# Reordered loads and casts, masks on VectorE and a one-hot last expert block in a hybrid conv, attention and MoE layer

## The chip, the cores and the metric

The kernel runs on the 8 cores of one Trainium2 chip. Each core computes one of the 8 batch elements by itself; nothing is exchanged. The metric is the device time in microseconds of the slowest core. Engines are named as in the profile: PE is TensorE (matmuls; PEld its weight loads), DVE is VectorE, ACT is ScalarE, POOL is GpSimd, SP is SyncE. Data come from HBM through 16 transfer engines per core. A transfer is issued from SP's queue or from POOL's; only POOL's can change the type, and the kernel uses it to load fp32 weights as bf16.

## What is computed

One layer of a diffusion backbone over 2048 latent tokens and 256 context tokens of width 1024:

```python
mod = silu(c) @ w_ada + b_ada            # shift, scale, gate for two sub-layers
h = rmsnorm(x) * (1 + sc1) + sh1         # and the same for the context tokens
b, cg, xin, q, k, v, ga, gb = split(h @ w_in)
ya = (b * conv3(cg * xin)) @ w_a         # gated short conv
yb = attention(q, k, v, window=128, context keys, sink) @ w_b
x = x + g1 * (sigmoid(ga) * ya + sigmoid(gb) * yb) @ w_o
h = rmsnorm(x) * (1 + sc2) + sh2
# MoE: the best of 4 groups, then the best 2 of its 8 experts
y = sum over the 2 experts of gate * (silu(h @ w_a[e]) * (h @ w_u[e])) @ w_down[e]
out = rmsnorm(x + g2 * y)
```

There are 32 experts; each has 1024 x 512 weights up and 256 x 1024 down, 3 MB in fp32. Both experts of a token lie in one group of eight.

## The kernel before

All work is recorded as operations of a small planner (class Sched, lines 38 to 380). Each has an engine, what it reads and writes, and an assumed cost; `order` runs a list scheduler over them, which at each moment starts, on every free engine, the oldest ready operation within a window of 300, and models two transfer rings. Its result is the fixed order of each engine's program, with semaphores between them. Engines run their programs strictly in order, so a transfer on POOL waits for everything ahead of it there. `weave` (line 381) mixes a main list of steps with a side list in proportion to given costs; `mix` (line 631) puts k cast steps among a list.

The stages, in order, for tokens in 4 chunks of 512 (16 tiles of 128):

- **Modulation** (lines 670 to 686): four 1 MB weights wad on POOL, x tiles 0 to 5 on SP.
- **First mixer stage** (lines 688 to 793): for each of 18 tiles `n1_step` normalises (square on ACT, scale on DVE, add on DVE or, for every third, POOL at line 699), transposes on PE and copies by ACT and DVE in turn into HT; `cx_step`, `proj_step` and `v_step` compute conv inputs, keys and values. `x_load` (line 606) fetches tile t+6 on SP when tile t is done, into 6 buffers.
- **Attention with conv** (lines 802 to 949): the six gate weights (wab, wsl 4 to 7; lines 802 to 804) are loaded; then q projections, `b_step` (three conv operations on DVE, one matmul, one multiply) and `mod2_step` (second modulation, with its own load) are woven with `att_steps`. `sc_step` multiplies the outer key blocks by a 0/1 mask on POOL (line 898).
- **Gates** (lines 964 to 1204): `gate_step` per chunk, woven with attention of chunks 2 and 3, the folding of g1 into w_o, `wo_step`, the second norm `n2_apply` (which writes the normalised rows to hd in HBM, line 1011) and routing.
- **Casts**: for 18 of the 32 experts the fp32 weights are copied to a bf16 tensor wbf in HBM beforehand, in 72 quarter steps (`pre_step`, line 622); quarter h waits for quarter h-3, the first three for the last x tile. PREK tells how many stand in each of five stages. The 18 are experts 6 to 15 and then every second one.
- **Routing end** (lines 1205 to 1266): ranks and one-hot tables give, per expert block of 256 token slots, the tokens to gather, the rows to scatter to and the gates.
- **Experts** (lines 1345 to 1435): 34 blocks in order (32 experts, 2 overflow blocks); the ring holds the weights of 6. Per block: `G` gathers 2 x 128 rows from hd (POOL), `T` transposes them on PE, `U` is up plus silu, `F` folds g2 into the down weights (DVE, line 1381), `Dn` is down with the gate on eviction, `O` scatters 2 x 128 rows into yd in HBM. `run_items` records them so that U(i), T(i+1) come before Dn(i-1), O(i-1), and the weights `W(i+5)` are loaded when block i-1 is done. Three further groups of overflow blocks lie behind branches (`emit_region`) and run only if an expert has more than 256 tokens.
- **Tail** (lines 1454 to 1494): yd holds for each token two neighbouring rows. `yload` (SP) brings a tile of both rows, 8 buffers, after all scatters. `sum_step` adds the two rows on PE through an identity, adds x on DVE and squares on ACT; `out_step` scales on DVE and stores.

## Time and profile before

| | us |
|---|---|
| median of 3 runs | 907.84 |
| lowest, highest | 907.0, 973.5 |
| the profiled execution, device time | 906.63 |
| its span in the trace (slowest core, core 2) | 904.7 |
| spans of the other cores | 882.5 to 897.1 |

The page of the profile gives busy time per engine, the span in slices with the granted clock of TensorE and the share of the transfer engines, the queues, the chain of work that ended last, the costliest groups of instructions, and the issued transfers with their time to landing. The trace behind it answers questions about a stretch, a line or an engine. A wait "A <- B" is time in which engine A stood idle until B released it. A transfer share of 1.0 means that all 16 engines were busy; matmul times are those of the pipeline and depend on the granted clock.

### The profile page before, as it was taken

How to read it: one execution, taken by the hardware profiler on the slowest of the kernel's cores; microseconds unless marked ns; L12 is line 12 of the kernel's file. 1: busy time of each engine (PE TensorE's matmuls, PEld its weight loads, DVE VectorE, ACT ScalarE, POOL GpSimd, SP SyncE). 2: the span in 40 equal slices, each digit the busy share in tenths (PEclk: the TensorE clock that was granted, in tenths of full speed). 3: DMA queues.
4: the chain of work that ended last, by engine and by line, in shares of the span. 5: the costliest groups of instructions: out<-in, count | busy, mean ns of one | idle time of the engine just before them, and what ended most of it. 6: DMA issues, size and time to landing. Idle time of an engine off the chain costs nothing. (4 is left out here: it accounts for less than half of the span.)

```text
span 904.7 us, 14299 instructions; the slowest of 8 cores (882.5 to 904.7 us)
## 1 busy us (share of the span) xinstructions
PE 751.6 (83%) x5494; PEld 422.5 (47%) x5494; DVE 532.2 (59%) x1054; ACT 379.1 (42%) x687; POOL 327.2 (36%) x383
## 2 busy tenths in 40 slices
PE   6887799898999999999999943899699959788461
PEld 2344455343455444454444422576476637556210
DVE  1548946799743656568698787644344334333197
ACT  2326422644466775424253341045245415344353
POOL 2021411335344754211211104267577637632200
PEclk9988999999999999999999965799899979989685
DMA  8994799999977899999988899379989999996498
GB/s 151 209 204 152 153 147 155 150 149 126 149 108 105 187 158 174 196 151 173 188 138 136 128 180 165 97 223 304 223 264 213 229 220 248 245 234 216 153 323 321
DMA packets 37007, 168.41 MB, mean 186 GB/s; under 512 B 11692, under 2 KB 13868, under 8 KB 28611
## 3 DMA queue, kind: packets, MB, share of 16 engines
q0 software_dynamic: 27136, 140.36, 80.6%
q1 hardware_dynamic: 9796, 27.06, 8.8%
q8 instruction: 46, 0.75, 0.4%
q14 instruction: 29, 0.24, 0.1%
HBM read 234.26 MB, written 58.72 MB: 324 GB/s over the span
## 5 line engine op out<-in xcount | busy, mean ns | idle before, releaser
L550 PE MATMUL ps<-sb 128*128 128x512 bf16 (+10 forms) x4452 | 685.8, 310 | 116.5 <-DVE sb L583 24.8
L550 PEld LDWEIGHTS ps<-sb 128*128 128x128 bf16 (+4 forms) x4452 | 361.9, 102 | 416.0 <-issue 79.1
L563 ACT ACTIVATE sb<-ps 128x512 bf16<-128x512 f32 (+4 forms) x385 | 211.2, 588 | 339.5 <-PE ps L550 247.6
L568 DVE TENSOR_TENSOR sb<-ps,sb 128x256 bf16<-128x256 f32 (+4 forms) x196 | 85.4, 446 | 159.3 <-PE ps L550 79.9
L563 ACT ACTIVATE sb<-ps,sb 128x512 bf16<-128x512 f32 x136 | 83.4, 687 | 53.1 <-PE ps L550 29.9
L1350 POOL DMA_INDIRECT sb<-hd,sb x68 | 74.7, 1098 | 77.3 <-PE ps L1362 49.6
L580 DVE SCALAR_TENSOR_TENSOR sb<-sb 128x1024 f32<-128x1024 f32 (+4 forms) x96 | 101.5, 1072 | 1.5
L1401 POOL DMA_INDIRECT yd<-sb x68 | 72.9, 1072 | 55.0 <-ACT sb L563 34.3
L565 ACT ACTIVATE sb<-sb 128x1024 bf16<-128x1024 f32 x50 | 52.8, 1055 | 89.6 <-DVE sb L568 56.1
L898 POOL TENSOR_TENSOR sb<-sb 128x512 bf16<-128x512 bf16 x60 | 66.7, 1121 | 61.4 <-ACT sb L563 61.0
L1381 DVE TENSOR_TENSOR sb<-sb 128x2048 bf16<-128x2048 bf16 x34 | 41.7, 1226 | 76.0 <-DMA sb<-wex 43.2
L568 DVE TENSOR_TENSOR sb<-sb 128x512 bf16<-128x512 f32 (+5 forms) x102 | 80.8, 798 | 1.4
L580 DVE SCALAR_TENSOR_TENSOR sb<-sb,ps 128x512 f32<-128x512 f32 (+2 forms) x74 | 47.8, 645 | 44.8 <-PE ps L550 35.4
L629 POOL DMA_DIRECT2D wbf<-wex x72 | 37.1, 517 | 99.4 <-DMA wbf<-wex 98.8
L568 DVE TENSOR_TENSOR sb<-sb,ps 128x512 f32<-128x512 f32 (+1 forms) x65 | 42.6, 677 | 30.4 <-PE ps L550 30.2
L583 DVE COPY sb<-ps 128x1024 bf16<-128x1024 bf16 (+3 forms) x84 | 53.1, 660 | 6.1 <-PE ps L550 4.3
L568 POOL TENSOR_TENSOR sb<-sb 128x1024 bf16<-128x1024 f32 x6 | 16.0, 2672 | 76.1 <-PE ps L709 41.2
L1362 PE MATMUL ps<-sb 128*128 128x128 bf16 x544 | 36.7, 220 | 2.5 <-DVE sb L583 2.5
L1362 PEld LDWEIGHTS ps<-sb 128*128 128x128 bf16 x544 | 33.6, 98 | 3.8 <-DVE sb L583 2.7
L577 DVE TENSOR_SCALAR sb<-sb 128x1 f32<-128x1 f32 (+4 forms) x54 | 16.2, 310 | 32.1 <-ACT sb L565 32.0
L571 DVE TENSOR_TENSOR sb<-sb 128x16 f32<-128x16 f32 (+9 forms) x62 | 31.2, 512 | 2.2 <-DMA sb<-wo 1.3
L563 ACT ACTIVATE sb<-sb 128x1 f32<-128x1 f32 (+5 forms) x52 | 13.3, 266 | 36.7 <-DVE sb L577 16.4
(52 smaller groups left out, 246.5 us busy)
## 6 DMA issues: line engine op xcount, KB each, us to landing
wbf<-wex POOLq DMA_DIRECT2D x72, 384.0 KB, 12.4
sb<-wbf POOLq DMA_DIRECT2D x18, 1536.0 KB
sb<-wex POOLq DMA_DIRECT2D x16, 1536.0 KB
sb<-wad POOLq DMA_DIRECT2D x12, 1024.0 KB, 21.2
sb<-x SPq DMA_DIRECT2D x16, 512.0 KB, 23.1
sb<-wsl POOLq DMA_DIRECT2D x8, 1024.0 KB, 32.6
sb<-x POOLq DMA_DIRECT2D x16, 512.0 KB, 12.4
sb<-yd SPq DMA_DIRECT2D x16, 512.0 KB, 12.8
```

The lines of the kernel that those rows point to most:

```text
L550: ins = e.matmul(o, lhsT=l, rhs=r, start=s0, stop=s1)
L563: S.op("act", lambda e: e.activation(out=out, in_=in_, func=func, scale=scale), reads=[in_] + list(extra), writes=w)
L565: S.op("act", lambda e: e.activation(out=out, in_=in_, func=func, accum_out=accum), reads=[in_], writes=w)
L568: S.op(eng, lambda e: e.tensor_tensor(out=out, in0=a, in1=b, op=op), reads=[a, b], writes=[out])
L580: S.op(eng, lambda e: e.scalar_tensor_tensor(out=out, in0=a, scalar=s, in1=b, op0=o0, op1=o1), reads=[a, b] + list(rd), writes=[out])
L583: S.op(eng, lambda e: e.tensor_copy(out=out, in_=a), reads=[a], writes=[out], fast=a.dtype == BF16)
L629: S.op("pool", lambda e: e.dma_start(out=o_, in_=i_), reads=[("wbf", h - PRED)] if h >= PRED else [("xl", 17)], writes=[("wbf", h)], dma=( ...
L898: S.op("pool", lambda e, p4=p4, m_=m_: e.tensor_tensor(out=p4, in0=p4, in1=m_.unsqueeze(1).to_broadcast([128, 4, 128]), op=ALU.mult), read ...
L1350: S.op("pool", lambda e, x_=x_, ix=ix: e.indirect_dma_start(out=x_, out_offset=None, in_=hd_d, in_offset=bass.IndirectOffsetOnAxis(ap=ix, ...
L1362: ins = e.transpose(psb[:, k * 128:(k + 1) * 128], x_[:, k * 128:(k + 1) * 128], identb)
L1381: S.op("dve", lambda e: e.tensor_tensor(out=wdv[r], in0=wdv[r], in1=G2b.unsqueeze(1).to_broadcast([128, 2, 1024]), op=ALU.mult), reads=[wd ...
L1401: S.op("pool", lambda e, q=q, ix=ix: e.indirect_dma_start(out=yd_d, out_offset=bass.IndirectOffsetOnAxis(ap=ix, axis=0), in_=YB[q], in_off ...
```

## The change

- **x loads**: tiles 6 to 17 are loaded by POOL instead of SP. All adds of the first norm are on DVE; three of four copies of a transposed tile are on ACT, one on DVE.
- **Casts**: the first three wait for x tile 8 instead of 17; ten stand among the steps of the first mixer stage, then 10, 16, 16, 14 and 6 in the five later ones.
- **Gate weights**: one load stands behind every fourth step of the attention stage's main list, between the second modulation's.
- **Conv**: its first operation is on ACT. **Masks**: on DVE.
- **Experts**: the order is all experts but 7, 15, 23, 31 (with the overflow blocks at 12 and 22), then these four. Cast are, of those after the first six, two of three, and the last four: still 18.
- **yd**: the first half of its rows holds a token's first expert, the second half its second; where the first is one of the four last ones the two are swapped (sign of the token number, array tks). Tokens of a tile are spread two by two, and hd is written accordingly.
- **Last block** (expert 31): not scattered. `Z` writes zero rows for its tokens, `last_tok` and `last_place` build a one-hot matrix PL from its token list, and `sum_step` adds it by two matmuls per half tile from SBUF.
- **End of the experts**: Dn and O of blocks 31 and 32 come before the next U; Dn of block 33 stands behind the branches. The yd loads (16 of 512 KB, each the rows of 256 tokens in one half) are recorded before the branches: three wait only for the first 30 blocks, the others for all but block 33. If an overflow group runs, it loads them again.
- **Sum**: for five tiles x is added on PE in fp32, squared by ACT and scaled by DVE from PSUM.
- **Planner**: a DVE operation with two large SBUF inputs is taken to wait for a running POOL operation; transfers still open at the branches stay in the model.

```diff
+XC = 8
...
-PREK = (14, 16, 16, 16, 10)
+PREK = (10, 16, 16, 14, 6)
...
+        two = eng == "dve" and sum(1 for k, c in rd if k is None and len(c) >= 64) >= 2
...
+                if o["two"]:
+                    ce += max(0.0, st["pb"] - t)
                 o["t"] = t
                 free[e] = t + ce
+                if e == "pool" and o["dma"] is None:
+                    st["pb"] = t + ce
...
-            sdma(xs[t % 6], src, ("xs", t % 6), also=[("xl", t)])
+            if t < 6:
+                sdma(xs[t % 6], src, ("xs", t % 6), also=[("xl", t)])
+            else:
+                gdma(xs[t % 6], src, ("xsg", t % 6), also=[("xl", t)])
...
-        pre = {e_: i_ for i_, e_ in enumerate(list(range(6, 16)) + list(range(17, 32, 2)))}
+        stat_e = [e_ for e_ in range(NE) if e_ % 8 != 7]
+        last_e = [7, 15, 23, 31]
+        prel = [e_ for i_, e_ in enumerate(stat_e[6:]) if i_ % 3 != 1][:NPRE - 4] + last_e
+        pre = {e_: i_ for i_, e_ in enumerate(prel)}
...
-            S.op("pool", lambda e: e.dma_start(out=o_, in_=i_), reads=[("wbf", h - PRED)] if h >= PRED else [("xl", 17)], writes=[("wbf", h)], dma=("wbf", h % PRED), cost=PREC)
+            S.op("pool", lambda e: e.dma_start(out=o_, in_=i_), reads=[("wbf", h - PRED)] if h >= PRED else [("xl", XC)], writes=[("wbf", h)], dma=("wbf", h % PRED), cost=PREC)
...
-            tt(xn[t % 2], x_, mod1[:, 2 * c, :], ALU.add, eng="pool" if t % 3 == 2 else "dve")
+            tt(xn[t % 2], x_, mod1[:, 2 * c, :], ALU.add)
...
-            if t % 2 == 0:
+            if t % 4 != 3:
...
-            weave(main, [(1.0, n1_step(t)) for t in nxt])
+            n1s = []
+            for t in nxt:
+                n1s.append((1.0, n1_step(t)))
+                if t >= XC:
+                    n1s.append((0.0, pre_step))
+            weave(main, n1s)
...
-        gdma(slotf(0), wab_d[0], ("w", 0), [("xl", 17)]); gdma(slotf(1), wab_d[1], ("w", 1), [("xl", 17)])
-        gdma(slotf(2), wsl_d[4], ("w", 2), [("xl", 17)]); gdma(slotf(3), wsl_d[6], ("w", 3), [("xl", 17)])
-        gdma(slotf(4), wsl_d[5], ("w", 4), [("xl", 17)]); gdma(slotf(5), wsl_d[7], ("w", 5), [("xl", 17)])
+        gate_src = [(0, wab_d[0]), (1, wab_d[1]), (2, wsl_d[4]), (3, wsl_d[6]), (4, wsl_d[5]), (5, wsl_d[7])]
+
+        def gate_load(n):
+            i, src = gate_src[n]
+            return lambda: gdma(slotf(i), src, ("w", i), [("xl", 17)])
...
-                ts(t_, UC[:, j, o0:o0 + 512], wcs[:, j * 3:j * 3 + 1], bcs[:, j:j + 1], ALU.mult, ALU.add, rd=[wcs, bcs])
+                u_ = UC[:, j, o0:o0 + 512]
+                S.op("act", lambda e: e.activation(out=t_, in_=u_, func=AF.Identity, bias=bcs[:, j:j + 1], scale=wcs[:, j * 3:j * 3 + 1]),
+                     reads=[u_, wcs, bcs], writes=[t_])
...
-                        S.op("pool", lambda e, p4=p4, m_=m_: e.tensor_tensor(out=p4, in0=p4, in1=m_.unsqueeze(1).to_broadcast([128, 4, 128]), op=ALU.mult),
-                             reads=[p_, m_], writes=[p_])
+                        S.op("dve", lambda e, p4=p4, m_=m_: e.tensor_tensor(out=p4, in0=p4, in1=m_.unsqueeze(1).to_broadcast([128, 4, 128]), op=ALU.mult),
+                             reads=[p_, m_], writes=[p_], cost=0.45)
...
+            if i % 4 == 3:
+                main.append((0.0, gate_load(i // 4)))
...
-        items = [("s", e_) for e_ in range(NE)]
+        items = [("s", e_) for e_ in stat_e]
...
+        items += [("s", e_) for e_ in last_e]
...
+                k8 = Kh[0][:, tl, :].rearrange("p t (g n) -> p t g n", n=8)[:, :, :, 7]
+                sg = smc(9)
+                S.op("dve", lambda e: e.tensor_reduce(out=sg, in_=k8, axis=AX.X, op=ALU.add), reads=[k8], writes=[sg], cost=0.2)
+                ts(sg, sg, -2.0, 1.0, ALU.mult, ALU.add)
+                ttb(tks[:, :, tl], tokc[:, :, tl], sg.unsqueeze(1).to_broadcast([128, 2, 4]), ALU.mult, [tokc[:, :, tl], sg])
...
+        def Z():
+            for s in range(2):
+                ix = rowi[0][:, s, LE:LE + 1]
+                S.op("pool", lambda e, ix=ix: e.indirect_dma_start(
+                    out=yd_d, out_offset=bass.IndirectOffsetOnAxis(ap=ix, axis=0),
+                    in_=YB[7], in_offset=None, bounds_check=2 * L - 1, oob_is_err=False),
+                    reads=[YB[7], ix], writes=[("yz", s)], dma=("yz", s), cost=0.8)
+
+        def last_tok():
+            tl_ = toki[0][:, :, LE]
+            cpy(tki, tl_)
+            for s in range(2):
+                ts(tkf[:, s, :], i32r[:, 0:8], -256.0, tki[:, s:s + 1], ALU.mult, ALU.add, rd=[tki])
+
+        def last_place(s):
+            def f():
+                io = i256.rearrange("p (n k) -> p k n", k=2).unsqueeze(1).to_broadcast([128, 8, 2, 128])
+                tk = tkf[:, s, :].unsqueeze(2).unsqueeze(3).to_broadcast([128, 8, 2, 128])
+                S.op("dve", lambda e: e.tensor_tensor(out=PL[s], in0=io, in1=tk, op=ALU.is_equal), reads=[rb, tkf[:, s, :]], writes=[PL[s]], cost=2.3)
+            return f
+
+        over_at[3].append(last_tok)
+        over_at[6] = [last_place(0)]
+        over_at[7] = [last_place(1)]
...
+        Z()
+        early = (NA - 2, NA - 3)
+
         def run_items(lo, hi):
+            nr_ = NRING if lo == 0 else 5
             for i in range(lo, hi + 1):
+                if i - 1 in early:
+                    Dn(i - 1)
+                    O(i - 1)
...
+        yord = [(0, 0), (1, 0), (2, 0), (0, 1), (1, 1), (2, 1)] + [(q, b) for q in range(3, 8) for b in range(2)]
+        ykey = [("xs", i) for i in range(6)] + ["c_cc", "c_sink", "c_bada", "c_ng1", "c_idf", "c_wc", "c_bc", "c_b2", "c_ng2", "c_brt"]
+        yq = {qb: view(W1 + ((12 + j) % 18) * 4096, 2048, BF16).rearrange("p (k n) -> p k n", n=1024) for j, qb in enumerate(yord)}
+
+        def yload(q, b, eng, ydk):
+            y_ = yq[q, b]
+            src = yd_d[b * L + q * 256:b * L + (q + 1) * 256, :].rearrange("(p k) n -> p k n", k=2)
+            S.op(eng, lambda e: e.dma_start(out=y_, in_=src), reads=ydk, writes=[y_, ("yl", q, b)], dma=ykey[yord.index((q, b))], cost=1.7)
...
+        ydk = [("yd", i, s) for i in range(NA - 1) for s in range(2)] + [("yz", s) for s in range(2)]
+        for q, b in yord:
+            yload(q, b, "sp", ydk if b or q > 2 else [("yd", i, s) for i in range(NA - 4) for s in range(2)])
...
+        Dn(NA - 1)
...
+        wide = (1, 4, 7, 10, 13)
+        held = {}
+
         def sum_step(t):
-            y_ = YT[t % NYT]
+            q, k_ = divmod(t, 2)
+            hb = []
             for h in range(2):
                 b_ = bank("main")
-                mm(b_[:], [(b_[:], identb, y_[:, k_, h * 512:(h + 1) * 512], k_ == 0, k_ == 1) for k_ in range(2)], [identb, y_])
+                hs = slice(h * 512, (h + 1) * 512)
+                ya = yq[q, 0][:, k_, hs]; yb = yq[q, 1][:, k_, hs]
                 xv = x1t(t)[:, 2 * h:2 * h + 2, :]
-                tt(xv, xv, q4(b_[:]), ALU.add)
-            if t + NYT < 16:
-                yload(t + NYT)
-            act(q4(junk2[t % 2]), x1t(t), AF.Square, accum=ss3[:, t:t + 1])
+                xl = [(q4(b_[:]), identf, xv, False, False)] if t in wide else []
+                mm(b_[:], [(b_[:], identb, ya, True, False), (b_[:], identb, yb, False, False)] + xl
+                   + [(b_[:], PL[s][:, q, k_, :], YLt[s][:, hs], False, s == 1) for s in range(2)],
+                   [identb, identf, ya, yb] + ([xv] if xl else []) + [PL[s][:, q, k_, :] for s in range(2)] + [YLt[s][:, hs] for s in range(2)])
+                if xl:
+                    act(junk2[t % 2][:, hs], b_[:], AF.Square, accum=s3h[:, h:h + 1])
+                    hb.append(b_)
+                else:
+                    tt(xv, xv, q4(b_[:]), ALU.add)
+            if hb:
+                tt(ss3[:, t:t + 1], s3h[:, 0:1], s3h[:, 1:2], ALU.add)
+                held[t] = hb
+            else:
+                act(q4(junk2[t % 2]), x1t(t), AF.Square, accum=ss3[:, t:t + 1])
...
-                stt(xu, xu, rstd3[:, u:u + 1], q4(FGt), ALU.mult, ALU.mult, rd=[rstd3[:, u:u + 1]])
+                if u in held:
+                    for h in range(2):
+                        stt(xu[:, 2 * h:2 * h + 2, :], q4(held[u][h][:]), rstd3[:, u:u + 1], q4(FGt)[:, 2 * h:2 * h + 2, :], ALU.mult, ALU.mult, rd=[rstd3[:, u:u + 1]])
```

## Rows read from the trace of the kernel before

**Rows 1.** The page: its first line, and TensorE's share in part 1

```profile
span 904.7 us, 14299 instructions; the slowest of 8 cores (882.5 to 904.7 us)
...
PE 751.6 (83%) x5494; PEld 422.5 (47%) x5494; DVE 532.2 (59%) x1054; ACT 379.1 (42%) x687; POOL 327.2 (36%) x383
```

**Rows 2.** Stretches: length; PE, PEld, DVE, ACT, POOL busy; clock, DMA share, GB/s

```profile
60.00:150.00 90.00, 78.15 (x530) 43.24 (x529) 59.08 (x88) 34.84 (x68) 22.79 (x24) 0.94 0.81 160
...
150.00:250.00 100.00, 89.65 (x774) 42.51 (x772) 85.14 (x147) 47.73 (x88) 36.15 (x41) 1.00 1.02 146
...
250.00:350.00 100.00, 99.58 (x858) 50.71 (x858) 51.08 (x99) 67.52 (x127) 55.54 (x69) 1.00 0.85 142
...
855.00:905.00 50.00, 21.51 (x64) 6.25 (x64) 40.70 (x66) 21.06 (x42) 0.00 (x0) 0.67 0.91 321
```

**Rows 3.** Stretches of 20 us, one at the hand-over

```profile
530.00:550.00 20.00, 9.94 (x52) 5.96 (x52) 15.72 (x79) 3.22 (x7) 3.73 (x5) 0.50 1.02 180
```

**Rows 4.** Stretches, before the first refill and the expert stage

```profile
570.00:590.00 20.00, 16.26 (x132) 12.18 (x132) 11.21 (x35) 2.05 (x5) 5.10 (x5) 0.83 0.25 71
...
590.00:810.00 220.00, 185.93 (x1580) 135.50 (x1577) 86.23 (x138) 90.28 (x170) 138.15 (x140) 0.94 0.95 242
```

**Rows 5.** Waits of TensorE, 60 to 110: us in total, times, longest

```profile
PE ps L709 <- DVE sb L568: 5.4, 1, 5.4
...
PE ps L550 <- ACT sb L563: 4.9, 1, 4.9
```

**Rows 6.** The page, part 6: transfers by line, KB each, us to landing

```profile
wbf<-wex POOLq DMA_DIRECT2D x72, 384.0 KB, 12.4
...
sb<-x SPq DMA_DIRECT2D x16, 512.0 KB, 23.1
...
sb<-wsl POOLq DMA_DIRECT2D x8, 1024.0 KB, 32.6
...
sb<-x POOLq DMA_DIRECT2D x16, 512.0 KB, 12.4
```

**Rows 7.** Instructions by line: 145 to 262 (VectorE, GpSimd), 60 to 150, the page

```profile
L580 DVE SCALAR_TENSOR_TENSOR sb<-sb 128x512 f32<-128x512 bf16 x28 | 28.5, 1037 | 0.1
...
L577 DVE TENSOR_SCALAR sb<-sb 128x512 f32<-128x512 bf16 x14 | 9.5, 703 | 0.0
...
L898 POOL TENSOR_TENSOR sb<-sb 128x512 bf16<-128x512 bf16 x29 | 33.0, 1147 | 30.6 <-ACT sb L563 30.3
...
L580 DVE SCALAR_TENSOR_TENSOR sb<-sb 128x512 f32<-128x512 bf16 x4 | 3.0, 753 | 0.1
...
L1381 DVE TENSOR_TENSOR sb<-sb 128x2048 bf16<-128x2048 bf16 x34 | 41.7, 1226 | 76.0 <-DMA sb<-wex 43.2
```

**Rows 8.** Timeline of ScalarE, the first tanh of the gates

```profile
236.91 2.06 ACT L563 ACTIVATE sb<-ps 128x512 f32<-128x512 f32 x4 [0.70 <-PE ps L550]
```

**Rows 9.** Timeline of GpSimd's issues, 480 to 550

```profile
505.89 0.53 POOL L629 DMA_DIRECT2D wbf<-wex  x1
...
545.31 1.06 POOL L540 DMA_DIRECT2D sb<-wex  x2 [15.61 <-DVE sb L583]
```

**Rows 10.** Timeline of TensorE: start, us, line, operation, tiles, count

```profile
115.00 3.62 PE L550 MATMUL ps<-sb 128*128 128x512 bf16 x16
...
547.75 2.08 PE L550 MATMUL ps<-sb 128*128 128x128 f32 x8 [1.17 <-DVE sb L580]
...
574.54 1.07 PE L1362 MATMUL ps<-sb 128*128 128x128 bf16 x16
...
834.87 9.02 PE L550 MATMUL ps<-sb 128*128 128x512 bf16 x54
```

**Rows 11.** The chain that ended last, its step to the first yd load

```profile
850.34 4.89 DMA sb<-yd
```

**Rows 12.** Instructions of VectorE by form, 855 to 905

```profile
L568 DVE TENSOR_TENSOR sb<-sb,ps 128x512 f32<-128x512 f32 x32 | 20.7, 679 | 15.7 <-PE ps L550 15.7
...
L580 DVE SCALAR_TENSOR_TENSOR sb<-sb 128x1024 f32<-128x1024 f32 x16 | 19.8, 1278 | 0.1
```

199 lines of the change are left out of this document (116 added, 83 removed).

## The prediction

> **What bounds the kernel now.** The profiled execution took 906.63 us, of which the trace covers 904.7 [rows 1]; the median of the runs shown is 907.84, 1.2 more, so I make the sum against 906.6 and add 1.2 at the end. I read the views in this order: the page's engine totals, the table of stretches, the waits inside the stretches with a gap, then the timelines at the two places where TensorE stands still.
>
> The totals say TensorE, 83% busy [rows 1], but that is a mean over stages with different limits. The table of stretches parts them. From 250 on TensorE is busy 99.58 of 100 us at full clock [rows 2], and it stays near that to the end of the gates: nothing that the change does to VectorE or the queues can win there. Before it, 60 to 150 leaves TensorE 12 us idle and 150 to 250 leaves it 10, the second with VectorE busy 85 of 100 [rows 2]. At 530 to 550 TensorE has half its time while the transfer engines are full (1.02) [rows 3]. In the expert stage, 590 to 810, the transfer engines are busy 0.95 of the time and TensorE 186 of 220 us [rows 4]: that stage is bound by transfers, not by matmuls. The tail, 855 to 905, has transfers at 0.91 and VectorE at 40.7 of 50 [rows 2]. So the reader should look for two things in this change: what it does to the order in which the transfer queue is used up, and what it does to the tail.
>
> **Part 1, the first mixer stage (60 to 150).** The x loads 6 to 17 go from SP to POOL, the norm's adds all go to VectorE, three of four copies to ScalarE, and ten casts start here. The gaps: TensorE waits 5.4 us for VectorE and 4.9 us for ScalarE [rows 5], both in tiles whose x came late or whose POOL add was slow. On SP an x load took 23.1 us to land; the same 512 KB on POOL later in the kernel took 12.4 [rows 6]. So the queue that is moved to serves them sooner, as long as they don't stand behind weights. Against that, the ten casts: a cast lands after 12.4 us with three in flight [rows 6], so one costs the queue about 4.1 us and ten cost 41; the stretch has 0.81 of its 90 us filled, 17 us free [rows 2], and four of the gate weights (1 MB each, 6.4 us at this stretch's 160 GB/s) that were issued here move later, which frees some 25 more. It fits, barely. Bounds: minus 12 (all the gaps go) to plus 24 (no room is freed: 41 less 17). I take minus 4: the waits for x go, the rest of the gaps stays.
>
> The Trainium skill, DMA: Bandwidth & Descriptors, Issuing engine by pattern, speaks against this move: a simple load belongs on Sync, which it calls generally faster than GpSimd. The rows above go the other way here; by the rule alone this part would be a loss, and it is the third rival below.
>
> **Part 2, attention with the conv steps (150 to 250).** Off POOL go 60 mask multiplies, 29 of them here at 1.15 us [rows 7]. On VectorE such a multiply isn't shown. Above, a 128x512 operation of VectorE takes 0.70 [rows 7]; below, a quarter of the 128x2048 bf16 multiply is 0.31 [rows 7]. I take 0.43, nearer the bf16 row since types and layout are the same: 29 x 0.43 = 12.5 us more for VectorE. Off VectorE goes the conv's first step to ScalarE, 14 here x 0.70 = 9.8 us [rows 7]. And 28 conv steps with two SBUF inputs take 1.04 us on average [rows 7], where the same steps without a POOL multiply beside them take 0.75 in the stretch before, which has no mask [rows 7]; with POOL empty that gives 28 x 0.3 = 8.4 back. Net VectorE: 12.5 - 9.8 - 8.4 = minus 6 of 85. ScalarE takes 14 x 0.7 = 10 us; it is busy 48 of 100 [rows 2], so that is covered; without the cover it would cost 10. Bounds: minus 10 (all of TensorE's gap) to plus 3 (no relief: 12.5 - 9.8). I take minus 4. The gate weights, now loaded one by one between the modulation weights, cost nothing while they land before the first gate's tanh, at 236.9 us [rows 8]; the work that hides it is this stage itself; the fourth rival is that cover gone.
>
> **Part 3, the hand-over to the experts (500 to 580).** Here TensorE waits for a chain: routing on VectorE, then the first gathers, then T(0) at 574.5 [rows 10]. The gathers stand on POOL behind the loads of experts 4 and 5, issued at 545.3 [rows 9], and those stand in a queue that is full [rows 3]. The last cast is issued at 505.89, with three more in the 15 us before it, among the first three expert loads [rows 9]. After the change 66 of the 72 casts are placed before the last gate stage instead of 62, and they start some 30 us sooner, so those four should be gone: 4 x 4.1 = 16.5 us of queue ahead of the gathers. Some of it turns into idle time, since the first expert loads can't go before the gates have freed their slots: I count minus 14. The routing grows by three small VectorE operations per chunk, of which the last chunk's lie on the path: 3 x about 0.3, as for the quarter multiply above, = plus 1. If the gathers were now issued ahead of experts 4 and 5, another 10 would go; I don't count that. Bounds: minus 25 to 0. I take minus 13.
>
> **Part 4, the expert stage.** The bytes don't change: 14 uncast experts and 18 cast ones before and after, six uncast ones first. Before, ten cast ones follow, then the two kinds alternate; after, about every third is uncast and four cast ones end it. Between 590 and 810 the transfer engines are free for 5% of 220, 11 us [rows 4], nearly all of it in the run of cast experts; in the second half they are full and TensorE stalls. Spreading the heavy loads can win those 11 and no more; the idle three quarters of 570 to 590 [rows 4], when the ring is full and no slot is free, stay. Bounds: minus 11 to plus 8 (the first heavy loads stall a queue that now has no easy run to recover in). I take minus 8. Two zero scatters, two 128x2048 compares on VectorE (2 x about 2.3 by the planner's own cost) and the earlier Dn(31) and Dn(32) lie in stretches where POOL and VectorE are under half busy: nothing.
>
> **Part 5, the tail.** Before: the last Dn ends at 834.87 + 9.02 = 843.9; the first yd load is issued at 850.34 and lands at 855.2 [rows 10, 11], the span ends at 904.7: 60.8 us. After: Dn(32) runs ahead of U(33) and its scatter is the last one that the loads wait for, block 33 being added from SBUF through a one-hot. The loads then go out about when Dn(33) ends, some 5.5 us sooner, and three of sixteen are already in. Then the summing: VectorE before 32 x 0.679 + 16 x 1.278 + 2.8 = 45 [rows 12]; after, with five tiles summed on TensorE, 22 x 0.679 + 11 x 1.278 + 10 x 0.69 (the wide tiles' half steps, as the adds) + 3.6 = 39.5 (2.8 and 3.6 are the small operations, some 0.2 per tile). Transfers: 16.8 MB at 321 GB/s [rows 2] is 52 us, after 15.2 MB, 47. TensorE goes from 64 matmuls to 128 and ten in fp32: at full clock 128 x 0.226 [rows 10] = 29, plus 5 for the fp32 ones (8 of 128 columns took 2.08 us at a granted clock of 0.50 [rows 3, 10], so 512 columns cost 1.04, half that at full), 34 in all: under the other two. So the summing gives 5 and the earlier start 5.5: minus 10. Bounds: minus 16 (the prefetched tiles count in full) to plus 16 (second rival).
>
> **Sum.** -4 - 4 - 13 - 8 - 10 = -39: 906.6 - 39 + 1.2 = 869.
>
> **The rivals.**
> 1. The bytes decide. The transfer engines move the same bytes, and what is cast earlier only pushes other transfers later. Then parts 3 and 4 give little (-4) and 1 and 2 nothing; the tail stays: 906.6 - 14 + 1.2 = 894. For it: 0.95 in the expert stage [rows 4]. Against it: the free 19% of 60 to 150 and 15% of 250 to 350 [rows 2].
> 2. The tail's clock. In the tail the granted clock is 0.67 [rows 2]. With twice the matmuls TensorE becomes the bound if the clock stays at 1.2 GHz: 128 x 0.45 + 10 x 1.04 = 68 us, plus 9 for the first load and the last store, 77 against 60.8: plus 16 where I have minus 10, 895. Against it: where TensorE was busy four fifths of the time the clock was mostly full (16.26 of 20: 0.83 [rows 4]).
> 3. The x loads behind the weights. On POOL they queue behind wsl, which takes 32.6 us to land [rows 6], 9.5 more than an x load on SP. The first ones come later by that, once: +9.5 for -4, 882. Decided by whether x6 is there before the wait that ends at 72.3 [rows 5].
> 4. On the other side: gate weights late. Gate loads share one in-order POOL queue with modulation loads and casts; a load of wsl took 32.6 us to land [rows 6]. If each of the six waits for the one before, 6 x 32.6 = 196 us from 150 on, the last lands at 346, needed about 260, some gates after the first [rows 8]: TensorE stands for 86, 869 + 86 = 955. It makes the kernel slower than 926 as soon as the last one lands after 317. Against it: they don't wait for each other, only for their slots, and most issue early.
>
> **How the numbers follow.** Mine 0.48 (own range 852 to 886), rival 1 0.15, rival 2 0.12, rival 3 0.12, rival 4 0.07, and 0.06 for a gain beyond mine (gathers first in part 3), below 852. The range 850 to 900 leaves out rival 4 and part of the last, and slips of the rest: about 0.2. About 2% (18 us) is what a measurement of this kernel can tell from no change: faster means below 889.7. Mine, rival 3, the gain beyond mine and about half of rivals 1 and 2, less a little, come to 0.77; slower is rival 4, 0.07; within 2% the rest, 0.16.
>
> **What would show it.** Part 1: the 5.4 and 4.9 us waits gone. Part 2: the conv steps at 0.75 us. Part 3: T(0) before 565 instead of 574.5. Part 4: no stretch of the expert stage under 0.9 after the first refill. Part 5: under 8 us between the last Dn and the first sum, at a clock over 0.8. I am wrong if the queue is as full at the hand-over as before (rival 1), or if a wait for wsl or wab appears at the gates.

## The result

| | before | after |
|---|---|---|
| ratio of the times, 95% interval | 1 | 0.971 (0.967 to 0.976) |
| median, us | 907.4 | 881.9 |
| span of the slowest core in the trace | 904.7 (core 2) | 880.2 (core 1) |
| spans of the other cores | 882.5 to 897.1 | 851.8 to 876.8 |

The change is 26 us faster; 39 were forecast (869, range 850 to 900). In some runs the cores of one die or of both show a lower granted clock and take longer: medians and ratios leave such runs out, and the means over the cores below leave out two such cores of the second copy of the changed kernel and four of the kernel with the masks on GpSimd, whose ratio is not read for that reason. The slowest core is another one after, and the cores differ by 28 us, so I follow the change by four marks taken from the timelines of each of the eight cores and averaged: the last store of hd (GpSimd), the first transpose T(0) of an expert block (TensorE), the end of the last Dn (its eviction on ScalarE), the end of the span.

| mean of the cores, us | before | after | difference | forecast |
|---|---|---|---|---|
| start to last store of hd (parts 1, 2) | 524.4 | 519.2 | -5.2 | -8 |
| last store of hd to T(0) (part 3) | 46.5 | 23.9 | -22.6 | -13 |
| T(0) to the last Dn (part 4) | 262.2 | 275.1 | +12.9 | -8 |
| last Dn to the end (part 5) | 58.9 | 48.5 | -10.4 | -10 |
| span | 892.0 | 866.7 | -25.3 | -39 |

The page of the profile after, first line and the busy times (to be held against [rows 1]):

```profile
span 880.2 us, 14399 instructions; the slowest of 8 cores (851.8 to 880.2 us)
...
PE 773.6 (88%) x5578; PEld 431.1 (49%) x5578; DVE 523.6 (59%) x1116; ACT 397.6 (45%) x719; POOL 254.5 (29%) x329
```

Stretches of the kernel after (length; PE, PEld, DVE, ACT, POOL busy; clock, DMA share, GB/s), against [rows 2 to 4]:

```profile
60.00:150.00 90.00, 87.14 (x609) 47.02 (x608) 65.71 (x103) 43.22 (x80) 16.77 (x32) 0.97 1.00 175
150.00:250.00 100.00, 90.36 (x790) 43.50 (x789) 72.96 (x161) 62.50 (x113) 8.14 (x16) 0.95 1.02 150
250.00:350.00 100.00, 100.00 (x849) 50.90 (x847) 57.02 (x132) 64.81 (x121) 17.39 (x34) 1.00 0.95 151
...
530.00:550.00 20.00, 14.98 (x87) 10.51 (x87) 9.49 (x39) 3.63 (x5) 12.95 (x13) 0.52 0.85 162
...
570.00:590.00 20.00, 20.00 (x160) 12.48 (x157) 13.69 (x34) 6.90 (x13) 11.63 (x13) 1.00 0.84 201
...
790.00:810.00 20.00, 19.53 (x168) 14.26 (x167) 9.53 (x15) 9.57 (x18) 5.68 (x6) 0.96 0.55 209
810.00:830.00 20.00, 12.18 (x88) 7.93 (x86) 4.03 (x7) 7.62 (x14) 5.65 (x5) 0.89 0.41 126
```

Read down the second column and the last but one. From 60 to 150 TensorE gained 9 us and the transfer engines went from 0.81 to full: the early casts use what stood free. From 150 to 250 TensorE gained only 0.7, though VectorE is 12 us less busy. These are two different cores; in the mean over the eight, TensorE stands idle 3.5 us instead of 9.5 in the first of the two stretches and 9.5 instead of 8.8 in the second. At 570 to 590 it works without a gap where before the transfer engines were busy only 0.25 of the time. At 790 to 830, where before they were nearly full up to 830, they now stand idle half the time.

The waits of TensorE in the first two stages (from 60 to 110, then from 150 to 250) say why the second stage gained nothing:

```profile
PE ps L587 <- DVE sb L620: 1.7, 1, 1.7
PE ps L587 <- ACT sb L600: 0.6, 1, 0.6
...
PE ps L587 <- DMA sb<-wad: 9.0, 1, 9.0
```

The longest ones of 150 to 250 in the kernel before:

```profile
PE ps L550 <- DVE sb L568: 3.2, 3, 1.5
PE ps L550 <- POOL sb L898: 2.8, 2, 2.2
```

The 5.4 and 4.9 us of [rows 5] are gone. In the attention stage the many short waits for VectorE and GpSimd, 9.4 us in all, are gone too, and one wait of 9.0 us for a weight of the second modulation stands in their place.

The hand-over, on GpSimd's timeline (issue, us, line, operation) and on TensorE's:

```profile
484.61 0.49 POOL L671 DMA_DIRECT2D wbf<-wex  x1 [2.71 <-DMA wbf<-wex]
...
534.10 1.08 POOL L1420 DMA_INDIRECT sb<-hd,sb  x1 [15.28 <-DVE sb L1221]
...
539.04 0.61 POOL L577 DMA_DIRECT2D sb<-wex  x1
...
542.21 0.61 POOL L577 DMA_DIRECT2D sb<-wex  x1
```

```profile
541.53 1.91 PE L1432 MATMUL ps<-sb 128*128 128x128 bf16 x16
...
573.92 6.02 PE L587 MATMUL ps<-sb 128*60 128x256 f16 x41
...
827.51 3.57 PE L587 MATMUL ps<-sb 128*128 128x512 bf16 x8 [6.41 <-POOLq L1568]
831.67 36.78 PE L587 MATMUL ps<-sb 128*128 128x512 bf16 x148 [0.59 <-DMA sb<-yd]
```

The last cast is issued at 484.6 instead of 505.9, and the gathers go out at 534.1 among the loads of experts 4 and 5, not behind them as in [rows 9]; T(0) follows 7.4 us after the first gather, where before it took 28. The row at 573.9 is the start of the overflow table's 32 matmuls (128 x 256 in f16; the row merges other matmuls into it): before they ran ahead of T(0). The row at 827.5 is the last block's Dn, behind the branches.

### The profile page after: what moved, and what is told of

It is laid out like the page before. It is cut to its first block, busy times and chain, and to the rows that moved or that the text cites. A ratio compares the mean times of both kernels' runs of the same rounds, so it can differ in the third digit from the quotient of the medians.

```text
span 880.2 us, 14399 instructions; the slowest of 8 cores (851.8 to 880.2 us)
## 1 busy us (share of the span) xinstructions
PE 773.6 (88%) x5578; PEld 431.1 (49%) x5578; DVE 523.6 (59%) x1116; ACT 397.6 (45%) x719; POOL 254.5 (29%) x329
## 4 chain that ended last, share of the span: by engine, by line
PE 64%; DMA 18%; DVE 9%; ACT 3%; issue 3%; another core or an unknown queue 1%; POOL 0%; SPq 0%; POOLq 0%; DVEq 0%; ACTq 0%
PE ps L587 59%; DMA sb<-wex 7%; DMA sb<-wad 4%; DMA sb<-x 4%; DVE sb L605 2%; PE ps L940 2%; PE ps L1432 2%; ACT sb L600 2%; DVE sb L617 2%; DMA wbf<-wex 2%; DVE sb L620 1%; DMA sb<-ng 1%; DVE sb L1451 1%; ACT sb L602 1%
## 5 line engine op out<-in xcount | busy, mean ns | idle before, releaser
L587 PE MATMUL ps<-sb 128*128 128x512 bf16 (+10 forms) x4536 | 706.8, 310 | 82.8 <-DVE sb L620 16.0
L587 PEld LDWEIGHTS ps<-sb 128*128 128x128 bf16 (+4 forms) x4536 | 369.9, 102 | 392.5 <-issue 102.5
L617 DVE SCALAR_TENSOR_TENSOR sb<-sb 128x1024 f32<-128x1024 f32 (+5 forms) x93 | 84.1, 913 | 4.0 <-ACT sb L899 2.5
L1496 POOL DMA_INDIRECT yd<-sb x66 | 72.3, 1096 | 48.8 <-ACT sb L600 27.7
L605 DVE TENSOR_TENSOR sb<-sb 128x512 bf16<-128x512 f32 (+6 forms) x113 | 81.2, 724 | 5.2 <-ACT sb L602 3.5
L602 ACT ACTIVATE sb<-sb 128x1024 bf16<-128x1024 f32 x45 | 47.5, 1056 | 72.3 <-DVE sb L605 40.7
L620 DVE COPY sb<-ps 128x1024 bf16<-128x1024 bf16 (+5 forms) x79 | 50.4, 660 | 11.3 <-PE ps L587 8.9
L605 DVE TENSOR_TENSOR sb<-sb,ps 128x512 f32<-128x512 f32 (+1 forms) x55 | 36.5, 678 | 27.0 <-PE ps L587 26.6
L577 POOL DMA_DIRECT2D sb<-x x26 | 14.8, 571 | 79.3 <-DVE sb L605 44.9
L940 PE MATMUL ps<-sb 64*128 64x512 bf16 x156 | 27.8, 387 | 0.2 <-ACT sb L600 0.2
L949 DVE TENSOR_TENSOR sb<-sb 128x512 bf16<-128x512 bf16 x60 | 24.2, 413 | 4.7 <-ACT sb L600 4.3
```

The costliest lines, as they stand in the source:

```text
L587: ins = e.matmul(o, lhsT=l, rhs=r, start=s0, stop=s1)
L602: S.op("act", lambda e: e.activation(out=out, in_=in_, func=func, accum_out=accum), reads=[in_], writes=w)
L605: S.op(eng, lambda e: e.tensor_tensor(out=out, in0=a, in1=b, op=op), reads=[a, b], writes=[out])
L617: S.op(eng, lambda e: e.scalar_tensor_tensor(out=out, in0=a, scalar=s, in1=b, op0=o0, op1=o1), reads=[a, b] + list(rd), writes=[out])
L620: S.op(eng, lambda e: e.tensor_copy(out=out, in_=a), reads=[a], writes=[out], fast=a.dtype == BF16)
L940: ins = e.matmul(o, lhsT=l, rhs=r, start=s0, stop=s1)
```

## The experiments

Each kernel is the changed one with one edit. The order of the instructions is planned anew from the edited list. Ratios are against the kernel before, run on the same chip. The marks are those of the table above, means over the cores, one profiled execution each.

| chip | kernel | ratio (interval) | last hd | T(0) | T(0) to last Dn | last Dn to end |
|---|---|---|---|---|---|---|
| A | changed | 0.971 (0.967 to 0.976) | 519.2 | 543.1 | 275.1 | 48.5 |
| B | four casts moved back | 0.969 (0.962 to 0.975) | 522.1 | 546.1 | 276.4 | 49.6 |
| B | experts 4, 5 before the gathers | 0.983 (0.977 to 0.988) | 522.2 | 565.3 | 268.6 | 49.0 |
| B | last three experts uncast | 0.964 (0.958 to 0.970) | 522.1 | 546.0 | 272.4 | 50.3 |
| B | x loads on SP | 0.975 (0.970 to 0.980) | 525.4 | 546.7 | 279.2 | 48.3 |
| C | changed, again | 0.969 (0.960 to 0.979) | 519.7 | 543.7 | 278.6 | 48.8 |
| C | no one-hot | 0.974 (0.967 to 0.982) | 521.4 | 545.5 | 272.0 | 56.0 |
| C | masks on GpSimd | 0.984 (0.973 to 0.995) | 523.7 | 544.7 | 277.4 | 49.8 |
| C | casts where they were | 0.981 (0.973 to 0.989) | 520.7 | 555.3 | 271.9 | 48.9 |
| D | modulation products later | 0.965 (0.960 to 0.970) | 519.9 | 543.8 | 276.4 | 48.6 |
| D | gate weights together | 0.969 (0.963 to 0.974) | 521.0 | 545.0 | 276.0 | 49.0 |
| D | old pattern of casts | 0.977 (0.972 to 0.982) | 520.5 | 544.5 | 281.4 | 50.0 |
| E | last three uncast, products later | 0.973 (0.968 to 0.977) | 520.8 | 544.7 | 271.2 | 50.5 |

Kernels with one letter ran one after the other on the same chip and are compared with each other; E is the chip of C at a later time. With the x loads on SP and with the masks on GpSimd, the planner put the first half of T(0) 2.6 us ahead of the second, elsewhere they stand together; those two rows are not compared by T(0). On B everything lies some 2.5 us later from the start on (first tanh of the gates 232.4 in a near copy of the changed kernel, 229.9 in the changed one on A).

> The changed kernel itself, beside the three below, so that each of them is compared with it on one chip: 0.971 of before, as measured (0.967 to 0.976).

The copy gives the same ratio, and its marks agree with the first to 1 us up to T(0) and to 3.5 in the stage: differences under that are not read below.

**The hand-over: experts 4 and 5 first.**

```diff
         W(3, [xhb(15)])
+        W(4, [xhb(15)])
+        W(5, [xhb(15)])
...
         G(1)
-        W(4, [toki[0]])
         G(2)
-        W(5, [toki[0]])
         G(3)
```

> The changed kernel with the loads of experts 4 and 5 recorded right behind that of expert 3, so that they stand ahead of the first gathers again. Both theories expect T(0) back from 543 to 560 to 572 us (mean of the cores). Theory A (the expert stage is a transfer queue: what is gained in front of it is given back while it waits for weights): the time stays at 0.971 of before, 0.965 to 0.977. Theory B (the 20 us won between the last store of hd and T(0) are the gain itself): they are lost again, ratio 0.990 or more.

The loads go out at 524.3, sixteen us ahead of the first gather (GpSimd's timeline, core 1):

```profile
524.33 1.71 POOL L577 DMA_DIRECT2D sb<-wex  x3 [0.16 <-issue]
540.14 1.08 POOL L1422 DMA_INDIRECT sb<-hd,sb  x1 [14.10 <-DVE sb L1221]
```

Against the kernel with four casts moved back, which ran beside it and is otherwise as the changed one, T(0) comes 19.2 us later and the median is 898.8 against 884.9, 13.9 more. By the mean span it is 10.8. So neither theory holds whole: more than half of what is won in front of T(0) stays won, the rest is given back between T(0) and the last Dn (268.6 against 276.4). From the last store of hd to T(0) it is 43.1 us with both loads ahead of the gathers and 24.0 with both behind them; in the kernel before, with both ahead, it was 46.5.

**The casts where they were.**

```diff
-PREK = (10, 16, 16, 14, 6)
+PREK = (14, 16, 16, 16, 10)
...
-XC = 8
+XC = 17
...
-                if t >= XC:
-                    n1s.append((0.0, pre_step))
```

> The changed kernel with the casts where they were: none before x tile 17, then 14, 16, 16, 16, 10. My step (four late casts stand in the queue ahead of the first gathers, 4 x 4.1 us): last cast 16 us later, T(0) 10 to 16 us later, 8 to 16 us slower at the end. Theory A: the later T(0) is half given back in the expert stage, as it was with experts 4 and 5 loaded first (19 us at T(0), 11 at the end): 4 to 8 us. A rival: the casts of the first stage hold up x tiles and modulation weights, so the mixer gains by their absence what the hand-over loses: within 2 us, with the 9 us wait for a modulation weight gone.

The last store of hd stays within 1.5 us of the changed kernel's, the last cast is issued at 493.8 instead of 487.5, where 16 us were expected (means of the same six cores), and T(0) comes 11.5 us later than in the copy beside it. The timelines of core 1, first TensorE's, then GpSimd's, show the wait itself, which the changed kernel hasn't, and what stands ahead of the first gather:

```profile
559.80 1.89 PE L1430 MATMUL ps<-sb 128*128 128x128 bf16 x16 [9.71 <-DMA sb<-hd,sb]
```

```profile
497.87 0.50 POOL L671 DMA_DIRECT2D wbf<-wex  x1
...
540.47 0.54 POOL L577 DMA_DIRECT2D sb<-wex  x1 [14.57 <-DVE sb L1219]
541.45 1.09 POOL L1418 DMA_INDIRECT sb<-hd,sb  x1 [0.44 <-issue]
```

It isn't a cast. The last cast of this core lands 16.0 us after its issue, at 513.9, and the first gather is issued at 541.5. What stands right ahead of the gathers is the load of expert 4: with the casts moved, the planner put it there, while in the changed kernel it stands behind the first four gathers. So this kernel has one of the two loads ahead of the gathers, and from the last store of hd to T(0) it takes 34.5 us, about halfway between 24.0 (none ahead) and 43.1 (both). In front of that load the queue is only some 2 us later than in the copy beside it: expert 3's load lands 23.8 us after the last store of hd, there 21.9 (means of the six cores). The edit therefore doesn't price the casts by themselves. Against the rival's expectation the wait for a modulation weight stays (8.9 us in the mean of the eight cores). At the end 5.5 of the 11.5 us are left by the mean span of the six cores, 8 by the medians (891.4 against 883.6).

**The expert stage: the old pattern of casts.** The order of experts stays; the cast ones stand at positions 6 to 15 and then at every second, as before.

```diff
-        prel = [e_ for i_, e_ in enumerate(stat_e[6:]) if i_ % 3 != 1][:NPRE - 4] + last_e
+        stat_l = stat_e + last_e
+        prel = stat_l[6:16] + stat_l[17::2]
```

> The changed kernel, its order of experts kept, with the cast ones where they stood before: positions 6 to 15 of the 32, then every second one. My step on the expert stage (spreading the heavy loads wins 8 us): 5 to 11 us slower, ratio 0.977 to 0.983, T(0) unchanged at 543 (mean). Theory A (the stage moves the same bytes whatever their order, and what it loses it loses in front and behind): ratio 0.969 to 0.973. A third way: the heavy loads at the end fill the idle 790 to 831, a little faster, 0.965 to 0.969.

The stage is 5 us longer than in the two kernels beside it (281.4 against 276.4 and 276.0), and the end 6 to 7 us later by the mean span, 8 to 11 by the medians (892.0 against 881.3 and 883.6). The stretches of this kernel (core 3) and, below them, the same ones of the changed kernel (core 1):

```profile
590.00:690.00 100.00, 88.69 (x748) 63.56 (x747) 48.94 (x83) 41.82 (x78) 67.63 (x63) 0.95 0.91 236
690.00:790.00 100.00, 79.24 (x621) 55.80 (x619) 34.05 (x54) 35.52 (x66) 56.03 (x57) 0.88 1.02 232
790.00:830.00 40.00, 29.16 (x233) 19.80 (x230) 13.46 (x21) 15.90 (x29) 11.63 (x11) 0.96 0.73 224
```

```profile
590.00:690.00 100.00, 88.72 (x748) 62.23 (x748) 47.09 (x86) 41.43 (x77) 67.20 (x65) 1.00 1.01 256
690.00:790.00 100.00, 78.81 (x641) 56.42 (x640) 38.19 (x59) 38.51 (x71) 58.33 (x60) 0.94 1.01 254
790.00:830.00 40.00, 31.71 (x253) 22.19 (x252) 13.55 (x22) 17.19 (x32) 11.33 (x11) 0.93 0.48 168
```

In the run of ten cast experts the transfer engines idle 9 us of 100; spread, they are full to 790 and are done sooner. That is the mechanism of part 4, with 5 us of the 8 that it counted.

**The last three experts uncast.** Since the transfer engines idle at the end, heavy loads could stand there:

```diff
-        prel = [e_ for i_, e_ in enumerate(stat_e[6:]) if i_ % 3 != 1][:NPRE - 4] + last_e
+        prel = [e_ for i_, e_ in enumerate(stat_e[6:]) if i_ not in (1, 5, 10, 14, 19)] + last_e[:1]
```

> The changed kernel with the last three experts (15, 23, 31) loaded uncast and three more of the middle ones cast instead; still 18 casts. The transfer engines have some 21 us of idle time between 790 and 831 and none between 590 and 790. Theory A (bytes in the full stretch decide): 3 x 7.1 us of transfers leave it, of which 8 to 18 us show: ratio 0.952 to 0.963. Theory B (the stage is set by its start, not by the order of casts): 0.971 as it stands. A rival to both: the late heavy loads stall the last blocks, ratio 0.98 or more, with waits of TensorE for weights behind 790.

The stage is 4.0 us shorter than in the kernel beside it, the median 880.9 against 884.9; the intervals overlap. TensorE's timeline of core 2 shows what takes the rest of the expected 8 to 18 us back: the late heavy loads are waited for.

```profile
787.47 5.23 PE L587 MATMUL ps<-sb 128*128 128x256 bf16 x32 [3.09 <-DMA sb<-wex]
800.44 6.87 PE L587 MATMUL ps<-sb 128*128 128x256 bf16 x38 [4.95 <-DMA sb<-wex]
810.23 4.96 PE L587 MATMUL ps<-sb 128*128 128x256 bf16 x38 [1.58 <-DMA sb<-wex]
```

**The first stage: x loads on SP.**

```diff
-                gdma(xs[t % 6], src, ("xsg", t % 6), also=[("xl", t)])
+                sdma(xs[t % 6], src, ("xsg", t % 6), also=[("xl", t)])
```

> The changed kernel with the x loads 6 to 17 on SP again, nothing else. My step (POOL serves them sooner; the waits for x at 67 to 72 and at 100 go because of it): waits of TensorE of 4 us and more come back between 60 and 110, the last store of hd comes 3 to 9 us later, ratio 0.973 to 0.981. The rule that I named as rival 3 (a simple load belongs on Sync): the x tiles land sooner, ratio 0.971 or less. A third way: the waits went because of the adds and copies, and the queue makes no difference, 0.971 and no wait of 4 us.

Transfers from 30 to 110 (KB each, median us from issue to landing) of this kernel, of the changed one and of the kernel before, then the waits of TensorE from 60 to 110 of this kernel:

```profile
sb<-x SPq DMA_DIRECT2D x10, 512.0 KB, 25.6
```

```profile
sb<-x POOLq DMA_DIRECT2D x10, 512.0 KB, 17.0
```

```profile
sb<-x SPq DMA_DIRECT2D x10, 512.0 KB, 16.1
```

```profile
PE ps L751 <- DVE sb L605: 7.1, 2, 6.2
PE ps L587 <- DVE sb L620: 1.3, 1, 1.3
```

With casts in the queue the same load lands in 25.6 us from SP and in 17.0 from POOL, and a wait for x of 6.2 comes back (ScalarE's square, the first step on that tile, waits 7.8 us for the load). The rule of the third rival doesn't hold here. But POOL is no sooner than SP had been without casts in that stretch, 16.1. The last store of hd is 3.3 us later than in the kernel beside it, which is near the first stage's term, -4; at the end it is 2.2 by the mean span and 4.8 by the medians, with overlapping intervals. The stage itself lost more. Stretches of this kernel, then of the kernel beside it (core 2 of each):

```profile
60.00:150.00 90.00, 72.48 (x445) 37.55 (x452) 53.55 (x81) 37.50 (x70) 10.96 (x22) 0.91 0.96 166
150.00:250.00 100.00, 96.84 (x831) 48.92 (x843) 79.97 (x160) 59.99 (x105) 10.20 (x20) 1.00 1.01 149
```

```profile
60.00:150.00 90.00, 82.81 (x582) 45.36 (x591) 62.35 (x97) 41.87 (x79) 15.49 (x30) 0.96 0.99 170
150.00:250.00 100.00, 87.67 (x750) 42.47 (x761) 73.01 (x158) 60.50 (x107) 8.03 (x16) 0.95 0.99 142
```

In the mean over the cores TensorE stands idle 14.9 us instead of 4.2 from 60 to 150, and 2.1 instead of 11.3 from 150 to 250, where no core waits for a modulation weight any more. What the loads on POOL win in the first stage, 10.7 us, is for the most part given back by that wait in the second.

**The masks on GpSimd.**

```diff
-                        S.op("dve", lambda e, p4=p4, m_=m_: e.tensor_tensor(out=p4, in0=p4, in1=m_.unsqueeze(1).to_broadcast([128, 4, 128]), op=ALU.mult),
-                             reads=[p_, m_], writes=[p_], cost=0.45)
+                        S.op("pool", lambda e, p4=p4, m_=m_: e.tensor_tensor(out=p4, in0=p4, in1=m_.unsqueeze(1).to_broadcast([128, 4, 128]), op=ALU.mult),
+                             reads=[p_, m_], writes=[p_])
```

> The changed kernel with the masks on GpSimd again. My step: the conv steps of VectorE with two SBUF inputs go from 0.75 back to about 1.04 us, the masks take 1.15 us each on GpSimd, TensorE waits some 3 us more for them between 150 and 250; 2 to 5 us slower than the changed kernel beside it at the last store of hd. Theory A (bytes decide what stands behind): less than 2 us at the end. A rival: that stage is held up by a modulation weight (the 9 us wait) and not by VectorE; no difference at the last store of hd either.

Instructions by form from 145 to 262, of this kernel (core 0), then of the changed one (core 1):

```profile
L949 POOL TENSOR_TENSOR sb<-sb 128x512 bf16<-128x512 bf16 x30 | 33.5, 1130 | 24.3 <-ACT sb L600 23.9
L617 DVE SCALAR_TENSOR_TENSOR sb<-sb 128x512 f32<-128x512 bf16 x28 | 26.1, 947 | 0.7 <-ACT sb L899 0.4
```

```profile
L617 DVE SCALAR_TENSOR_TENSOR sb<-sb 128x512 f32<-128x512 bf16 x28 | 20.4, 747 | 1.2 <-ACT sb L899 1.0
...
L949 DVE TENSOR_TENSOR sb<-sb 128x512 bf16<-128x512 bf16 x32 | 12.9, 411 | 3.4 <-ACT sb L600 3.2
L899 ACT ACTIVATE sb<-sb 128x512 f32<-128x512 bf16 x14 | 11.3, 817 | 15.1 <-DVE sb L605 15.0
```

The prices of part 2 hold: 0.747 us for a conv step with GpSimd nearly empty (8 of 100 us busy), 0.95 with its multiplies beside it, 0.41 for a mask on VectorE, 1.13 on GpSimd. On the same four cores the last store of hd is 3.9 us later than in the copy beside it, but the first tanh of the gates isn't (229.9 against 230.2): the gain comes behind 230, where the other half of the masks is, and not in the stage for which I counted it. At the end the mean span of those cores is 2 us longer. The ratio, 1.4% worse with wide intervals, is not read.

**The wait for the modulation weight.** Two tries. Four casts moved to later stages:

```diff
-PREK = (10, 16, 16, 14, 6)
+PREK = (6, 18, 18, 14, 6)
```

> The changed kernel with four casts moved from the attention stage to the two stages behind it (6, 18, 18, 14, 6). Both theories expect the 9.0 us wait of TensorE for a modulation weight at 208 to 217 to shrink below 4 us and the last store of hd to come 4 to 9 us earlier than 519.2 (mean). Theory A: the time falls by less than a third of that, ratio 0.967 to 0.972. Theory B: it falls by all of it, ratio 0.960 to 0.966.

The wait stays, 10.1 us: 19 instead of 20 casts are issued up to 226, since a cast is issued as soon as the third one before it has landed, wherever it stands in the list. The edit changed hardly anything, and so tells nothing about casts; it serves as a second copy. The other try leaves the loads and moves the products:

```diff
-            if i % 4 == 1:
+            if i in (1, 5, 9, 15, 19, 23):
                 main.append((2.5, mod2_step(i // 4)))
```

> The changed kernel with the fourth, fifth and sixth product of the second modulation two steps later in the list of the attention stage (behind steps 15, 19, 23 instead of 13, 17, 21); no load moves ahead. The fourth waits 9.0 us for its weight, issued at 181.5 and used at 217. All theories: that wait shrinks below 3 us. If it is the bound of that stage, the first tanh of the gates comes 5 to 9 us sooner than 229.9 (mean) and the last store of hd 4 to 8 sooner than 519.2; at the end half of it (as for the other shifts of T(0)), 2 to 5 us, ratio 0.965 to 0.969. If the queue is what the stage waits for, the wait only moves to the next weight and the first tanh stays: ratio 0.971.

The waits of TensorE from 150 to 250, and from 250 to 520 (core 3):

```profile
PE ps L587 <- DMA sb<-wad: 4.7, 1, 4.7
...
PE ps L587 <- DMA sb<-wad: 2.7, 1, 2.7
```

Half of the wait goes and another part of it moves to the next weight. The first tanh of the gates comes 9 us sooner than in the changed kernel (221.0 against 229.9, means; 230.8 and 232.4 in the two kernels beside it), as expected if that wait bounds the stage, but nothing of it is left at the last store of hd, 519.9. The median is 881.3, as the changed kernel's.

**The gate weights together**, ahead of the stage's list, as before the change:

```diff
+        for n in range(6):
+            gate_load(n)()
...
-            if i % 4 == 3:
-                main.append((0.0, gate_load(i // 4)))
```

> The changed kernel with the six gate weights recorded together ahead of the attention stage's list, as before the change. My step: they land in time either way, so no difference from this alone; but six of 6 us each then stand ahead of the modulation weights and casts of that stage: the wait for a modulation weight grows from 9.0 to 15 us or more, 2 to 6 us slower, ratio 0.973 to 0.978. If they only trade places with casts: ratio 0.969 to 0.973. A rival: the modulation weights then have the queue to themselves from 175 on and the 9.0 us wait goes: ratio 0.963 to 0.968.

No difference that these runs show (883.6 against 881.3 beside it): gate loads and casts trade places in a queue that is full either way. The wait for the modulation weights is 6.7 us in the mean over the cores, 8.5 in the changed kernel; it didn't grow to 15.

**The tail: no one-hot.** Block 33 is scattered like the others; its zero rows, its one-hot and its 64 matmuls go.

```diff
-                yb = YLt[s] if i == NA - 1 else YB[(i % 4) * 2 + s]
+                yb = YB[(i % 4) * 2 + s]
...
-        Z()
...
-                if i > lo and i - 1 not in early and i != NA:
+                if i > lo and i - 1 not in early:
...
-        ydk = [("yd", i, s) for i in range(NA - 1) for s in range(2)] + [("yz", s) for s in range(2)]
+        ydk = [("yd", i, s) for i in range(NA) for s in range(2)]
...
-        Dn(NA - 1)
```

> The changed kernel with block 33 scattered to yd like the others: no zero rows, no one-hot, no 64 matmuls for it in the sums; thirteen of sixteen yd loads wait for its scatter. My step (the loads go out 5.5 us sooner because they don't wait for the last block): 4 to 7 us slower than the changed kernel beside it. A rival: TensorE, busy without a break for 36.8 us in the tail after the change, is the bound there; without the 64 matmuls (14.5 us) the sums are bound by VectorE, which gives back most of the later start: within 2 us.

TensorE of core 2 waits 10.6 us between the last Dn and the first sum, 0.6 in the changed kernel:

```profile
826.03 2.04 PE L587 MATMUL ps<-sb 128*128 128x512 bf16 x8 [0.28 <-DVE sb L605]
838.63 12.76 PE L587 MATMUL ps<-sb 128*128 128x512 bf16 x36 [10.56 <-DMA sb<-yd]
```

On the same six cores the tail is 6.8 us longer (55.6 against 48.8), but the stage before it is 4.8 us shorter (273.7 against 278.5), since the last Dn no longer stands behind the branches. From T(0) to the end that makes 2.1 us, by the medians 3; the intervals overlap. So the wait that the one-hot removes is real, but most of what it wins behind the last Dn is paid ahead of it.

**Both edits that pointed down, together** (the last three experts uncast, the products later):

> Both edits that pointed down, together: the products of the second modulation two steps later (0.965 alone) and the last three experts uncast (0.964 alone); the changed kernel stood at 0.971 and 0.969. If they add, ratio 0.956 to 0.962, with the wait for a modulation weight under 5 us and T(0) to the last Dn 3 us shorter than 275.1 (mean). If what the first wins is given back in front of the experts, as its last store of hd at 519.9 says, only the second counts: 0.962 to 0.967. If neither was more than the scatter of the runs: 0.968 to 0.972.

The median is 884.5, where 883.6 was the changed kernel's on the same chip earlier. The stage is 4 us shorter, as with the first edit alone, and nothing adds: no version here beats the changed kernel by more than the scatter of its runs.

## Why the prediction was near in time and wrong in its parts

The forecast of the sum came within 13 us partly by luck: part 3 won 10 us more than counted, by a mechanism that was left out of the sum, and part 4 lost 21.

**Parts 1 and 2 (-8; measured -5.2).** In part 1 the two waits went, and the loads on SP again cost 3.3 us at the last store of hd. But its reason, that POOL serves the loads sooner than SP did, fails: in that stretch they landed in 16.1 us from SP before and land in 17.0 from POOL after; the 23.1 that I took is the median of all sixteen, those at the start among them. The move to POOL keeps the early casts from holding the loads up (25.6 from SP). What took the two waits away, the adds, the copies or the order of issue, no run separates, nor a weight load that the change also lets go two x tiles sooner. In part 2 the instruction prices held (ScalarE's first conv step took 0.82, not 0.70), but the cover didn't: TensorE gained 0.7 us in that stage, since a weight of the second modulation came late. It was issued at 181.5 behind two gate weights of 1 MB (165.6 and 174.8) and casts, and landed at 217. That is near rival 4's mechanism, with 9 us instead of 86, and on a neighbour of the weights that I had looked at. Which of the loads ahead makes it late is not shown: it stays with the gate weights together (6.7 us) and with the casts where they were (8.9), and goes with the x loads on SP. No gate weight was waited for.

**Part 3 (-13; measured -22.6).** Its step failed, though the time fell. The 14 us counted for four late casts are not there: with the loads of experts 4 and 5 ahead of the gathers, it takes 46.5 us from the last store of hd to T(0) with the old casts (the kernel before) and 43.1 with the new ones, so 3.4 us are left for the casts and all else. What I left out as a side case, the gathers ahead of experts 4 and 5, took place, and is worth 19.1 of the 22.6 (43.1 to 24.0). The change doesn't write that order down, the planner chooses it: with the old casts it puts one of the two loads back in front, and that, not casts in the queue, is most of the 11.5 us which that kernel loses at T(0).

**Part 4 (-8; measured +12.9) is the step that failed in sign.** The pattern of casts did win most of what was counted (5 us of the stage, 6 or more at the end). But I priced the stage as if its start were fixed. Three things came into it with the earlier T(0). Part of an earlier start is given back while the transfers catch up: 7.8 of 19.2 us with experts 4 and 5 first, which for 27.8 would be 11 (an estimate; with only expert 4 first it is 6.4 of 11.5). The overflow table's matmuls, 7.2 us ahead of T(0) before, are 9.4 us behind it after (means). And the last Dn now waits for the branches, 6.0 us on average, which the change's own text said and I costed at nothing; without it, in the kernel with no one-hot, the stage is 4.8 us shorter. With the pattern that makes 11 + 9.4 + 6.0 - 5 = 21, more than the 12.9; they can't simply be added, since the table's matmuls may fill time in which TensorE would wait for weights, and since with experts 4 and 5 first a part of the table (some 3 us) stands ahead of T(0) and so within the first term. The table was not tested by itself.

**Part 5 (-10; measured -10.4).** The sum agrees, but by a mark that moved: the last Dn itself comes up to 6.0 us later because of the branches, which shortens the tail and is in part 4's loss. Parts 4 and 5 together, from T(0) to the end, gave +2.5 where -18 was forecast. By terms:

```profile
L587 PE MATMUL ps<-sb 128*128 128x512 bf16 x129 | 30.4, 384 | 0.6 <-DMA sb<-yd 0.6
L587 PE MATMUL ps<-sb 128*128 128x512 f32 x20 | 10.2, 591 | 0.0
```

These are the matmuls of the changed kernel from 831 to 881. TensorE is busy without a break for 36.8 us, where I had 34: the ten fp32 products stand in the trace as twenty, 10.2 us instead of 5. The clock was 0.98 from 831 to 869, so rival 2 fell.

**The rivals.** Rival 1 (bytes) gave -4 for parts 3 and 4, I had -21; -9.7 was measured, between the two. It was right that the stage stays full (1.01 from 590 to 790), wrong that an order can't win there. Rival 3 fell with the loads on SP, rival 4 in size.

**What would have shown it.** T(0) before 565 (541.5; by the order of the loads, not by the casts), conv steps at 0.75, under 8 us between the last Dn and the first sum (0.6) came as said. "No stretch of the expert stage under 0.9" failed at 790 to 830 (0.55, 0.41): four cast experts at the end leave the transfer engines idle while TensorE works off the ring. Heavier loads there won back no more than 4 us.

**Open**: why half of the modulation wait, once gone, shows at the first tanh and nowhere at the last store of hd; where behind the first tanh the masks win their 3.9 us; how the stage's 12.9 us divide between transfers, table and branch; and what the casts cost at T(0) with the order of the loads held fixed.

## What to carry to other kernels

Where a stage's end is set by transfers, an earlier start is a gain only in part; count what it brings along (work that stood ahead of it, waits behind a branch) in the same sum. In an in-order queue that is full, look first at what stands ahead of the few small transfers for which everything waits: here two weight loads ahead of the gathers were worth 19 us at the first use and 11 to 14 at the end, the work moved between engines in the first two stages at most 5. And an entry moved in a list that a planner reorders has to be looked for in the trace before it is called a cause: four casts that were moved went out when they had before, and with the casts put back a weight load had moved in front of the gathers as well.
